# Experts: last four jobs written out, the first two slot chunks summed into tokens between them, final adds in a row

## The chip, the cores and the metric

One core of one Trainium2 chip runs the whole program. The metric is the device time of one execution in microseconds. The kernel is written by hand, with one instruction stream for each engine: TensorE (PE) multiplies matrices, VectorE (DVE) and ScalarE (ACT) do elementwise work, GpSimd (POOL) does a little, and SyncE (SP) issues nearly all transfers. Semaphores are all that ties the streams together. Matrix products land in eight PSUM banks, called pb[0] to pb[7], and everything else lies in SBUF.

## The reference, condensed to what matters

256 tokens of width 1024 go through two transformer blocks of two layers each. The second block ends each of its two layers (called l = 0 and l = 1) with a mixture of 32 experts, in groups of 8. This is the part that the change touches:

```python
e = grp[:, None] * EXPERTS_PER_GROUP + top_local          # two experts for each of 256 tokens
y_e = (silu(x_e @ w_gate[e]) * (x_e @ w_up[e])) @ w_down[e]   # 1024 -> 512 -> 1024
x = x + sum over the two experts of gate * y_e
```

The weights of one expert are three fp32 matrices of 2 MB each. After l = 0 comes the mixer of the next layer, which begins with a projection of the new x. After l = 1 comes a last rmsnorm, and its result is the output.

Which expert a token gets depends on the inputs. On the inputs of `setup_inputs()`, the reference's router, evaluated by itself, gives these numbers of tokens to experts 0 to 31 (each row sums to 512):

```
l = 0: 16 14 5 8 21 10 9 17 15 14 18 12 16 20 15 10 15 27 15 11 7 21 7 23 15 29 6 29 20 15 32 20
l = 1: 9 13 16 4 14 7 12 17 28 35 39 12 21 20 48 29 5 8 6 10 12 0 6 1 18 8 22 25 14 13 26 14
```

No expert has more than 64, and in l = 1 one expert, number 21, has none.

## The kernel before, in words

**Slots and jobs.** The 512 pairs of token and expert are sorted by expert into 512 slots. A job is one pass of one expert over a window of W = 64 slots that begins at the expert's first slot; what a job writes past its own slots, the next job writes over. `route` counts the tokens of each expert (`cm`), and `wm` is the number of jobs of each of 33 bins (32 experts, and one for what expert 0 has over 64). `wm` starts as "count over 0", or 1 where the bin's number is below `FORCED`, and grows with each further 64 tokens. FORCED = FIXED + 2 = 20: bins 0 to 19 get a job whether or not a token chose them. The sum of `wm`, less a constant, is read into the register `more` on every engine.

**Steps.** In step j PE multiplies job j's window by the gate matrix (`products` with m = 0, in two halves) and by the up matrix (m = 1), turns job j-1's gate and up results (`turn`), turns job j-2's result (`results`), and multiplies job j-1's hidden values by its down matrix (`down`). Order on PE: turn, gate half 0, turn, gate half 1, results, up, down. Steps 0 to 17 (FIXED = 18) are written out, with a planner that lays their weights out in three groups of buffers. Then a loop (`Fori(0, more)`) runs the steps from 18 on, one step more is written out (`step(more, last=True)`), and then comes `end`, in which only the rest of the last jobs is done.

**Weights.** From the loop on, weights go into `raw`, six buffers of 1 MB: one pair for gate, one for up, one for down. SP issues one 2 MB transfer for each matrix (L763), in the order gate, up, down. It issues a gate's after PE has used up the last gate of that pair, and likewise for the others, which the semaphore `used` counts. The last down comes as two transfers of 1 MB (L760, L761), into the gates' pair.

**Slots back to tokens.** The results stand turned in `ysT`. They are turned back in four chunks of 128 slots. For a chunk c: PE turns it in two halves of 4 transposes (`slots_turned(c)`, L1964) into `slot_bank(half, c)`, which is pb[6], pb[7] for c = 0 and c = 1, pb[0], pb[1] for c = 2 and pb[4], pb[5] for c = 3; ACT scales it by the gate values and rounds it (`slots`, L1252); DVE writes the rest that the rounding left (`low_slots`, L2772). Then PE sums the slots into tokens by a product with the 0/1 matrix `selT` (`into_tokens`, L2027), 2 matmuls of 128x512 for each half of the columns, half of the tokens (NT = 2) and chunk, so 8 for a chunk and 32 for a layer. In the kernel before, all four chunks add up in pb[0] to pb[3], and DVE then adds these four banks to `h` (L2808). Chunk 0 is turned at the start of the last step, chunk 1 in it ahead of `down`, chunks 2 and 3 in `end`. All 32 sums stand after the last `down`.

**After that.** In l = 0 PE turns `h` in two halves (`turn_half(8, 0)`, and `turn_half(8, 1)` inside `project` after its first 12 matmuls), DVE makes the low parts of the first mixer weights (`split_to`, L2119) and of the turned `h` (`evac_half`, L2130), and PE goes on with `project` (L1366). In l = 1 ACT squares `h` in four quarters (L1338), POOL makes the root, DVE multiplies by the gain (`with_gain`, L2816) and then by the root (L2862), and three transfers write the output.

## Time and profile before

| | |
|---|---|
| runs of the kernel before | 1877.14, 1872.03, 1872.38 us; median 1872.38 |
| the profiled execution's own time | 1876.49 us |
| its span, first to last instruction | 1874.7 us |
| mean granted TensorE clock | 0.99 |
| PE busy | 1784.4 us, 95% |
| DVE busy | 847.4 us, 45% |
| ACT busy | 705.3 us, 38% |
| moved by transfers | 549.37 MB, mean 293 GB/s |
| share of the chain that ended last | PE 72%, DMA 20%, DVE 4%, ACT 1%, POOL 1%, issue 1% |

The span is the time between the first and the last instruction of one profiled execution, and its own time, 1.8 us more, includes what lies around it. "Busy" of PE is the time in which matmuls were in flight, so a PE that is busy all the time need not be at its peak. The chain that ended last follows the work back from the last instruction, at each step to what released it; what is not on it had time to spare. The experts of l = 0 run from about 847 to 1306 us of the span, those of l = 1 from about 1418 to 1862 us.

### The profile page before, as it was taken

Reading aid. Unit: us, or ns where it says so; the run is one execution under the profiler, and the core shown is the slowest. Engines: PE = TensorE matmul, PEld = TensorE weight load, DVE = VectorE, ACT = ScalarE, POOL = GpSimd, SP = SyncE. Lnnn points to the kernel's source line nnn. Section 1 sums busy time; section 2 is a strip of 40 time slices with the busy share of each in tenths; the row PEclk is TensorE's granted clock in tenths of the full one; section 3 lists DMA queues with packets and bytes.
Section 4 is the critical chain, followed back from the end, with each engine's and each line's share of the span. In section 5 each row is a group of like instructions: output and inputs, shape, how many; then the busy total and the mean of one; then the engine's idle time right before and its main releaser. Section 6 shows DMA issues by size and latency. Waiting matters only on the chain.

```text
span 1874.7 us, 26258 instructions
## 1 busy us (share of the span) xinstructions
PE 1784.4 (95%) x10171; PEld 1142.2 (61%) x10171; DVE 847.4 (45%) x1532; ACT 705.3 (38%) x1205; POOL 105.6 (6%) x148
## 2 busy tenths in 40 slices
PE   8999999998999999999999898889999999988887
PEld 6779998886699997975334333334985334333333
DVE  4766556668765657874111111114785112111113
ACT  5554333656643335543222222223543222222223
POOL 3330000112200000010000000000010000000000
PEclk9999999998999999999999999999999999999999
DMA  9645555552256554558999999999648999999995
GB/s 319 205 155 189 180 180 179 165 184 79 94 166 200 180 180 135 180 224 368 428 428 427 427 421 425 429 428 370 198 171 368 425 427 428 427 426 424 428 429 226
DMA packets 130589, 549.37 MB, mean 293 GB/s; under 512 B 8030, under 2 KB 67768, under 8 KB 103480
## 3 DMA queue, kind: packets, MB, share of 16 engines
q1 hardware_dynamic: 127080, 539.53, 73.4%
q0 software_dynamic: 3088, 8.10, 1.4%
q8 instruction: 70, 1.15, 0.3%
q10 hardware_dynamic: 320, 0.34, 0.1%
q14 instruction: 31, 0.25, 0.0%
HBM read 546.83 MB, written 1.11 MB: 292 GB/s over the span
## 4 chain that ended last, share of the span: by engine, by line
PE 72%; DMA 20%; DVE 4%; ACT 1%; POOL 1%; issue 1%; SPq 0%; POOLq 0%; DVEq 0%; ACTq 0%
PE pb L1366 29%; DMA raw<-in_w_expert_down 16%; PE pb L1928 12%; PE pb L1955 10%; PE pb L1661 6%; DMA spare<-in_w_expert_gate 3%; PE pb L1936 2%; PE pb L1495 1%; PE pb L1472 1%; PE pb L1518 1%; PE pb L1595 1%; PE pb L1945 1%; POOL rms L903 1%; DVE parts L2119 1%; PE pb L1378 1%
## 5 line engine op out<-in xcount | busy, mean ns | idle before, releaser
L2119 DVE TENSOR_TENSOR parts<-raw,parts 128x2048 fp32r<-128x2048 f32 (+1 forms) x138 | 307.2, 2232 | 109.2 <-ACT parts L923 106.3
L923 ACT ACTIVATE parts<-raw 128x2048 fp32r<-128x2048 f32 (+1 forms) x138 | 256.5, 1867 | 210.5 <-PE pb L1366 154.1
L1366 PE MATMUL pb<-xT,parts 128*128 128x256 f32 (+1 forms) x2712 | 333.3, 283 | 0.0
L1366 PEld LDWEIGHTS pb<-xT,parts 128*128 128x128 f32 (+1 forms) x2712 | 329.2, 191 | 4.7 <-issue 2.9
L1928 PE MATMUL pb<-raw,xw 128*64 128x512 f32 x1360 | 319.5, 601 | 11.6 <-DMA raw<-in_w_expert_gate 11.6
L2739 DVE TENSOR_TENSOR qk<-qk,pb 128x256 f32<-128x256 f32 x126 | 53.1, 421 | 585.2 <-ACT qk L1235 585.0
L1366 PE MATMUL pb<-parts,xT 128*128 128x512 f32 (+1 forms) x1200 | 272.7, 386 | 3.0 <-DVE xT L2130 1.5
L1366 PEld LDWEIGHTS pb<-parts,xT 128*128 128x128 f32 x1200 | 218.4, 190 | 49.3 <-issue 4.4
L1230 ACT ACTIVATE qk<-pb 128x512 f32<-128x512 f32 x126 | 75.2, 597 | 302.8 <-PE pb L1928 302.8
L1928 PEld LDWEIGHTS pb<-raw,xw 128*64 128x64 f32 x1360 | 86.8, 136 | 153.7 <-issue 125.2
L1955 PE MATMUL pb<-raw,qk 128*64 128x512 f32 x624 | 142.8, 596 | 30.7 <-DMA raw<-in_w_expert_down 30.7
L1936 PEld LDWEIGHTS pb<-cst,qk 128*128 128x128 f32 x504 | 70.5, 209 | 97.3 <-issue 97.3
L1661 PE MATMUL pb<-parts,hidT 128*128 128x512 f32 x528 | 124.3, 391 | 3.1 <-DVE hidT L2356 3.1
L1955 PEld LDWEIGHTS pb<-raw,qk 128*64 128x64 f32 x624 | 47.1, 136 | 120.0 <-issue 119.7
L1928 PE MATMUL pb<-spare,xw 128*64 128x512 f32 x464 | 111.8, 614 | 4.8 <-DMA spare<-in_w_expert_gate 4.8
L1661 PEld LDWEIGHTS pb<-parts,hidT 128*128 128x128 f32 x528 | 97.7, 188 | 23.3 <-DVE hidT L2356 3.9
L1235 ACT ACTIVATE qk<-pb 128x256 f32<-128x256 f32 x126 | 48.3, 383 | 167.1 <-PE pb L1936 162.7
L1246 ACT ACTIVATE qk<-pb 128x512 f32<-128x512 f32 x63 | 37.6, 597 | 167.4 <-PE pb L1955 167.4
L1936 PE MATMUL pb<-cst,qk 128*128 128x128 f32 x504 | 93.5, 309 | 0.0
L2755 DVE COPY work<-pb 128x512 f32 x63 | 43.6, 692 | 62.1 <-PE pb L1945 62.1
L1955 PE MATMUL pb<-spare,qk 128*64 128x512 f32 x272 | 61.7, 594 | 4.6 <-DMA spare<-in_w_expert_down 4.6
L1928 PEld LDWEIGHTS pb<-spare,xw 128*64 128x64 f32 x464 | 30.0, 138 | 54.0 <-issue 45.9
(335 smaller groups left out, 1583.0 us busy)
## 6 DMA issues: line engine op xcount, KB each, us to landing
raw<-in_w_expert_gate SPq DMA_DIRECT2D x41, 2048.0 KB, 10.0
raw<-in_w_expert_up SPq DMA_DIRECT2D x37, 2048.0 KB, 10.8
raw<-in_w_expert_down SPq DMA_DIRECT2D x35, 2048.0 KB, 10.7
spare<-in_w_expert_down SPq DMA_DIRECT2D x16, 2048.0 KB, 15.9
spare<-in_w_expert_up SPq DMA_DIRECT2D x14, 2048.0 KB, 16.5
raw<-in_w_ffn_gate SPq DMA_DIRECT2D x22, 1024.0 KB, 5.3
raw<-in_w_ffn_up SPq DMA_DIRECT2D x22, 1024.0 KB, 5.3
raw<-in_w_ffn_down SPq DMA_DIRECT2D x22, 1024.0 KB, 4.9
```

What stands on the lines that cost most here:

```text
L923: nc.scalar.activation(parts[:, (SPL0[seg] + k) % SPL, 0, 0:kk * nn], raw[:, place, 0:kk * nn], ACT.Copy).then_inc(hi_done[seg], 1)
L1230: nc.scalar.activation(dst, pb[bank][:], ACT.Copy).then_inc(done[l], 1)
L1235: nc.scalar.activation(dst.rearrange("p (k s) -> p k s", k=4), pb[2 + m][:].rearrange("p (k i s) -> p k i s", k=4, i=2)[:, :, 0, :], ACT.C ...
L1246: nc.scalar.activation(ys, pb[4][:], ACT.Copy).then_inc(ys_done[l], 1)
L1366: ins = mm(out_ap, b if flip else a, a if flip else b, start=first and n == 0, stop=last and n == 2)
L1661: ins = mm(pb[2 * c + t][:], hidT[:, j, i, P * t:P * (t + 1)], w[p][:, j, 512 * c:512 * (c + 1)], start=(q == 1 and j == 0 and n == 0), st ...
L1928: ins = mm(pb[m][rows, :], xw[:, 4 * hf + k, :], w[:, k, :], start=(hf == 0 and k < 2), stop=(hf == 1 and k >= 2))
L1936: ins = nc.tensor.transpose(pb[2 + m][:, P * q:P * (q + 1)], view(src, q, [[DE // P, P]]), ident)
L1955: ins = mm(pb[4][W * c:W * (c + 1), :], ehj[:, 2 * hf + k, :], w[:, k, 512 * c:512 * (c + 1)], start=(hf == 0 and k == 0), stop=(hf == 1 a ...
L2119: v.tensor_tensor(two[:, 1, :], raw[:, place, 0:kk * nn], two[:, 0, :].bitcast(F32), ALU.subtract)\
L2739: v.tensor_tensor(d, d, pb[2 + m][:].rearrange("p (k i s) -> p k i s", k=4, i=2)[:, :, 1, :], ALU.add)\
L2755: v.tensor_copy(ysT2[:, :, :, bass.ds(s0, W)], pb[6][:].rearrange("p (q c s) -> p c q s", q=4, c=2))\
```

## The change

- `REST = 4` steps are written out behind the loop (before: one), on SP, ACT, PE and DVE. `more` is smaller by 3 for the same number of jobs. `FORCED` becomes FIXED + REST + 1 = 23.
- In the four steps, numbered 0 to 3: step 0 turns chunk 0 at its start, step 1 sums it; step 2 turns chunk 1 at its start, step 3 sums it. `TURNS` and `SUMS` hold this.
- New on PE, `sums(sc, half)`: 4 matmuls for one half of the columns of chunk sc, into pb[5] and pb[7]. Half 0 stands ahead of the step's `down`, half 1 behind it; half 1 of chunk 1 stands in `end`, between `down`'s second half and `slots_turned(2)`. Each waits until DVE has added the one before it.
- New on DVE, `add_part(sc, half)`: two adds of 128x512 from pb[5] and pb[7] into `h`, at the end of the step (half 1 of chunk 1 after `hidden` of `end`).
- `slots_turned(1)` waits in addition until both parts of chunk 0 are added, because pb[7] serves both.
- `into_tokens` covers chunks 2 and 3 alone (16 matmuls): chunk 2's first half around `results(end, 1)`, then `slots_turned(3)`, then chunk 3.
- The four final adds stand in a row. In l = 0 `split_to` and `evac_half`, which stood between the second and the third, come after the fourth. In l = 1 `with_gain(0)`, which stood between the third and the fourth, comes after the fourth.

```diff
-FORCED = FIXED + 2
+REST = 4
+FORCED = FIXED + REST + 1
...
+        TURNS, SUMS = {0: 0, 2: 1}, {1: 0, 3: 1}
...
+                for ahead in range(1, REST):
+                    job_weights((more, ahead))
+                end = (more, REST)
...
+                def sums(sc, half):
+
+                    pe.wait_ge(yt_v, 8 * l + 2 * sc + 2)
+                    if sc or half:
+                        pe.wait_ge(part_added, 4 * l + 2 * sc + half)
+                    for t in range(NT):
+                        for i in range(2):
+                            ins = mm(pb[5 + 2 * t][:], selT[:, sc, P * t:P * (t + 1)],
+                                     y_slots(half)[:, i, 512 * sc:512 * (sc + 1)], start=(i == 0), stop=(i == 1))
+                    ins.then_inc(sums_ready, 1)
+
...
-                    if last:
+                    if turned_chunk is not None:
                         pe.wait_ge(yadd_done[l], at(j, 1, -1))
-                        slots_turned(0)
+                        if turned_chunk:
+                            pe.wait_ge(part_added, 4 * l + 2)
+                        slots_turned(turned_chunk)
...
-                    if last:
-                        pe.wait_ge(yadd_done[l], at(j, 1, 0))
-                        slots_turned(1)
+                    if summed is not None:
+                        sums(summed, 0)
                     down(j, 1, down_at(False), range(1 if last else 2))
+                    if summed is not None and not last:
+                        sums(summed, 1)
...
-                step(more, last=True)
-                end = (more, 1)
+                for n in range(REST):
+                    step((more, n), TURNS.get(n), SUMS.get(n), n == REST - 1)
+                end = (more, REST)
                 turn(end, 1, 0, gs, gs_done)
                 turn(end, 1, 1, us, us_done)
-                down(more, 1, down_at(False), range(1, 2))
+                down((more, REST - 1), 1, down_at(False), range(1, 2))
+                sums(1, 1)
+                pe.wait_ge(yadd_done[l], at(end, 1, -1))
                 slots_turned(2)
-                pe.wait_ge(yt_v, 8 * l + 4)
                 results(end, 2)
                 down(end, 1, down_at(True))
...
                 for t in range(NT):
-                    into_tokens(0, t, 0)
+                    into_tokens(0, t, 2)
                 results(end, 1)
-                for sc in (1, 2):
-                    for t in range(NT):
-                        into_tokens(0, t, sc)
+                for t in range(NT):
+                    into_tokens(1, t, 2)
                 pe.wait_ge(yadd_done[l], at(end, 1, 1))
                 slots_turned(3)
-                for sc in range(3):
-                    into_tokens(1, 0, sc)
-                for t in range(NT):
-                    into_tokens(0, t, 3)
-                for sc in range(3):
-                    into_tokens(1, 1, sc)
+                for half in range(2):
+                    for t in range(NT):
+                        into_tokens(half, t, 3)
                 if l == 0:
                     turn_half(8, 0)
-                into_tokens(1, 0, 3)
-                into_tokens(1, 1, 3)
...
+                def add_part(sc, half):
+
+                    dve.wait_ge(sums_ready, 4 * l + 2 * sc + half + 1)
+                    if sc:
+                        dve.wait_ge(part_added, 4 * l + half + 1)
+                    for t in range(NT):
+                        hh = h[:, t, 512 * half:512 * (half + 1)]
+                        ins = v.tensor_tensor(hh, hh, pb[5 + 2 * t][:], ALU.add)
+                    ins.then_inc(part_added, 1)
...
-                add(0, 0)
-                add(0, 1)
+                for c in range(2):
+                    for t in range(NT):
+                        add(c, t)
...
```

## Rows read from the trace of the kernel before

**Rows 1.** GB/s moved in each fortieth of the span, 46.9 us each.

```profile
GB/s 319 205 155 189 180 180 179 165 184 79 94 166 200 180 180 135 180 224 368 428 428 427 427 421 425 429 428 370 198 171 368 425 427 428 427 426 424 428 429 226
```

**Rows 2.** Windows: us, busy by engine (instructions), clock, DMA share, GB/s.

```profile
1598.00:1831.00 233.00, 208.75 (x962) 77.01 (x958) 36.72 (x80) 56.54 (x113) 0.00 (x0) 0.99 1.01 426
```

**Rows 3.** Line L1230, two per job, in the experts of l = 0.

```profile
L1230 ACT ACTIVATE qk<-pb x64: 597/597/598, 854.3 to 1289.4; 128x512 f32<-128x512 f32 x64
```

**Rows 4.** The same line in the experts of l = 1.

```profile
L1230 ACT ACTIVATE qk<-pb x62: 597/597/599, 1425.4 to 1845.2; 128x512 f32<-128x512 f32 x62
```

**Rows 5.** Chain that ended last, two jobs of the written-out steps: start, us, what.

```profile
970.11 3.58 PE pb L1928 x16
...
982.80 3.58 PE pb L1928 x16
```

**Rows 6.** Timeline of SP: start, us, engine line; last regular jobs of l = 1.

```profile
1820.58 0.33 SPq L763 DMA_DIRECT2D raw<-in_w_expert_down  x1
1826.23 0.34 SPq L763 DMA_DIRECT2D raw<-in_w_expert_gate  x1
1830.26 0.33 SPq L763 DMA_DIRECT2D raw<-in_w_expert_up  x1
```

**Rows 7.** Page, DMA issues: KB each, median us to landing.

```profile
raw<-in_w_ffn_down SPq DMA_DIRECT2D x22, 1024.0 KB, 4.9
```

**Rows 8.** Timeline of PE, l = 1, last three steps and end: [idle before].

```profile
1820.34 0.75 PE L1936 MATMUL pb<-cst,qk 128*128 128x128 f32 x4
1821.56 1.94 PE L1928 MATMUL pb<-raw,xw 128*64 128x512 f32 x8 [0.48 <-DMA raw<-in_w_expert_gate]
...
1826.56 3.65 PE L1928 MATMUL pb<-raw,xw 128*64 128x512 f32 x16
1831.45 3.65 PE L1955 MATMUL pb<-raw,qk 128*64 128x512 f32 x16 [1.23 <-DMA raw<-in_w_expert_down]
1835.03 1.09 PE L1964 MATMUL pb<-cst,work 128*128 128x128 f32 x8
...
1836.54 1.94 PE L1928 MATMUL pb<-raw,xw 128*64 128x512 f32 x8
...
1846.15 1.94 PE L1955 MATMUL pb<-raw,qk 128*64 128x512 f32 x8
...
1857.12 0.60 PE L1945 MATMUL pb<-cst,qk 128*128 128x128 f32 x4
...
1859.41 1.03 PE L1964 MATMUL pb<-cst,work 128*128 128x128 f32 x8
1860.20 4.84 PE L2027 MATMUL pb<-parts,selT 128*128 128x512 f32 x20
```

**Rows 9.** Timeline of DVE, l = 1, end.

```profile
1857.86 0.69 DVE L2755 COPY work<-pb 128x512 f32 x1 [3.29 <-PE pb L1945]
...
1862.35 1.28 DVE L2808 TENSOR_TENSOR h<-h,pb 128x512 f32<-128x512 f32 x2 [0.17 <-PE pb L2027]
...
1865.41 1.22 DVE L2816 TENSOR_TENSOR qk<-h,qk 128x1024 f32<-128x1024 f32 x1
...
1869.45 0.75 DVE L2862 TENSOR_SCALAR xs<-qk,rms 128x1024 f32<-128x1024 f32 x1 [0.96 <-POOL rms L903]
```

**Rows 10.** Timeline of ACT, l = 1: squares of h.

```profile
1867.27 0.63 ACT L1338 ACTIVATE xs<-h 128x512 f32<-128x512 f32 x1 [1.13 <-DVE h L2808]
```

**Rows 11.** Chain that ended last, from the end of l = 0 into the mixer.

```profile
1306.47 1.28 DVE h L2808 x2
1307.75 2.20 DVE parts L2119
1309.95 1.58 DVE xT L2130 x4
...
1311.58 3.00 PE pb L1366 x12
...
1315.46 13.93 PE pb L1366 x84
```

More of the change, by code:

```diff
@@ L1278, in moe @@
                     step(j)
-                step(more, last=True)
-                end = (more, 1)
-                slots(1)
+                for n in range(REST):
+                    step((more, n), TURNS.get(n))
+                end = (more, REST)
                 first_parts(end, 1, 0, eg)
@@ L2012, in moe @@
                     step(j)
-                step(more, last=True)
-                end = (more, 1)
+                for n in range(REST):
+                    step((more, n), TURNS.get(n), SUMS.get(n), n == REST - 1)
+                end = (more, REST)
                 turn(end, 1, 0, gs, gs_done)
                 turn(end, 1, 1, us, us_done)
-                down(more, 1, down_at(False), range(1, 2))
+                down((more, REST - 1), 1, down_at(False), range(1, 2))
+                sums(1, 1)
+                pe.wait_ge(yadd_done[l], at(end, 1, -1))
                 slots_turned(2)
-                pe.wait_ge(yt_v, 8 * l + 4)
                 results(end, 2)
@@ L2027, in into_tokens @@
                         ins = mm(pb[2 * half + t][:], selT[:, sc, P * t:P * (t + 1)],
-                                 y_slots(half)[:, i, 512 * sc:512 * (sc + 1)], start=(sc == 0 and i == 0),
+                                 y_slots(half)[:, i, 512 * sc:512 * (sc + 1)], start=(sc == 2 and i == 0),
                                  stop=(sc == 3 and i == 1))
@@ L2773, in low_slots, with step @@
                             .then_inc(yt_v, 1)
-                def step(j, last=False):
+                def add_part(sc, half):
[6 more added lines that the diff above has]
+                    ins.then_inc(part_added, 1)
+                def step(j, turned_chunk=None, summed=None, last=False):
                     later = not isinstance(j, int) or j > 1
-                    if last:
-                        low_slots(0)
+                    if turned_chunk is not None:
+                        low_slots(turned_chunk)
                     if not later and j:
@@ L2787, in step @@
                         to_slots(j, 2)
+                    if summed is not None:
+                        add_part(summed, 0)
+                        if not last:
+                            add_part(summed, 1)
                 for j in range(FIXED):
@@ L2794, in moe @@
                     step(j)
-                step(more, last=True)
-                end = (more, 1)
-                low_slots(1)
+                for n in range(REST):
+                    step((more, n), TURNS.get(n), SUMS.get(n), n == REST - 1)
+                end = (more, REST)
                 sums(end, 1)
-                hidden(end, 1, at(more, 6, 4))
+                hidden(end, 1, at((more, REST - 1), 6, 4))
+                add_part(1, 1)
                 low_slots(2)
```

55 lines of the change are left out of this document (26 added, 29 removed).

## The prediction

> **What bounds the kernel now.** I read four views, from coarse to fine. The slices of the page come first: in both expert parts the GB/s row stands flat at 421 to 429 [rows 1], and the window over the late jobs of l = 1 gives 426 GB/s with all sixteen engines' share full, while PE is busy for 209 of 233 us [rows 2]. So the transfers bound this stretch. An early job, whose weights were loaded ahead, shows what PE needs by itself: the up products begin at 970.11 and again at 982.80, so 12.69 us a job [rows 5]. A late job takes 14.70 us: `down` begins at 1831.45 and then at 1846.15 [rows 8]. One job's weights are 3 x 2.097 = 6.29 MB, and at 426 GB/s that is 14.8 us, the same number. PE has 2.0 us to spare in a late step, and the timeline shows where: 1.23 us idle ahead of `down`, 0.48 us ahead of the first gate product and some more inside the turn before it, all released by a transfer [rows 8].
>
> The end of a layer is different. From 1831.45 on PE is hardly idle, and from 1856 to 1865 it only turns and sums slots [rows 8]. DVE's adds follow, then the squares, the root and the output [rows 9, 10]. So there are two kinds of place: steps in which PE's work is free up to 2.0 us, and an end in which it is paid.
>
> **The largest part: one more job.** FORCED goes from 20 to 23, so bins 20, 21 and 22 get a job even when no token chose them. The trace gives the jobs of each layer: line L1230 runs twice a job, 64 times in l = 0 and 62 times in l = 1 [rows 3, 4], so 32 and 31 jobs. With at most 64 tokens an expert, 31 jobs means one expert of 20 to 31 without a job. The trace doesn't say which; the reference's router says 21, with 0 tokens. It is now forced, and l = 1 has 32 jobs. l = 0 keeps its 32. The new job's window is written over by the next, so it only costs time: 6.29 MB in a stretch that the transfers bound. There is no cover for it, since the row of GB/s has no gap in it. I take 14.7 us. The lower bound is PE's 12.69 us [rows 5]; it would hold only if the transfers were ahead. The upper bound from the slowest full slice, 421 GB/s [rows 1], is 14.9 us.
>
> The Trainium skill (DMA: Bandwidth & Descriptors, Specifications) gives about 358 GB/s as a core's limit from HBM. By it the job would cost 17.6 us. The trace disagrees, with 426 GB/s held for 233 us [rows 2].
>
> **Steps 0 to 2, written out.** A step out of the loop issues the same transfers in the same order, and PE's written-out steps run at 12.69 us without a gap [rows 5], so being written out costs nothing. The moved work is what counts.
>
> Step 0 turns chunk 0 first. The kernel before does the same in its last step, and there the gate products begin 1.51 us after `down`'s end (1835.03 to 1836.54) instead of 1.22 (1820.34 to 1821.56) [rows 8]: 0.3 us late, which the 1.23 us ahead of `down` swallows. Cost 0.
>
> Step 1 sums half of chunk 0 ahead of `down`. Twenty such matmuls take 4.84 us [rows 8], so four take 0.97; this fits into the 1.23 us. The other half comes behind `down` and is followed at once by step 2's turning of chunk 1, which waits until DVE has added that half, since both use pb[7]. So PE goes through 0.97 (sums), 1.28 (two adds, as two take [rows 9]), some 0.2 for two handovers (one shows as 0.17 [rows 9]), 1.02 (turning) and 0.49 (the turn of the gates; 1.51 less 1.02): 3.96 us, where steady state begins the gate products after 1.22. Queued behind that wait are all of step 2's products. They start 2.8 us late. About 1.3 us of that goes into the idle time ahead of `down`, so `down` of step 2 is 1.5 us late. In step 3 the gates' idle time of 0.7 takes it to 0.8, and the first sum of chunk 1 adds 0.97 against 1.3: `down` of step 3 is 0.4 us late. Bounds for this: 0 (the handovers overlap) and 2.8 us (no idle time takes any).
>
> **The queue of loads.** SP's gate load of step 2 waits for products that are 2.8 us late. In steady state it is issued at 1826.23 [rows 6], while the `down` transfer issued at 1820.58 still has until about 1831.3 to land. A 1 MB load with nothing before it lands in 4.9 us [rows 7]; 2.5 of these are its bytes at 426 GB/s, so 2.4 are fixed, and a 2 MB one would need 7.3. Issued at 1829.0 it would land at 1836.3, and the gate products of a steady step begin 14.70 after 1821.56, at 1836.26. So it is just in time, and I take 0; the upper bound is the full 2.8 us.
>
> **What the last step saves.** It loses the turning of two chunks, 2 x 1.02 us. But its `down` began at 1846.15, exactly 14.70 after the one before, although both turnings stood ahead of it [rows 8]: it waited for its weights anyway. So this removal is worth 0, and the 0.4 us of lateness stands.
>
> **The end, up to the adds.** PE is without idle time from here. `sums(1, 1)` adds 0.97 ahead of `slots_turned(2)`, so the last `down` ends 0.4 + 0.97 = 1.4 us late. `results(end, 1)` keeps four sums ahead of it, and comes 1.4 late too. DVE's copy then ended at 1858.55 [rows 9] and ends at 1859.95; the last chunk is turned behind it. Before, PE was still busy with eight sums until 1859.41 [rows 8], so the turning moves by only some 0.45 us. From there on the old kernel's first adds, at 1862.35, came 0.17 us after DVE had ended its last `low_slots` [rows 9]: DVE's chain, not PE, set them. They move by the same 0.45. The sixteen removed sums, 16 x 0.24 = 3.9 us, are thus mostly work that hid behind DVE and ACT. Bounds: 0.45 later and 2.5 us earlier (3.9 less 1.4).
>
> **The adds in a row, l = 0.** Before: two adds, the split (2.20), the evacuation (1.58), and PE's `project` begins at 1311.58 and then has no gap for 18 us [rows 11]. Now two more adds, 1.4 us, stand ahead of the split. So `project` begins 0.45 + 1.4 = 1.85 us later, and all behind it moves. Bounds: -2.5 and +3 us.
>
> **The adds in a row, l = 1.** Before, the fourth add came after `with_gain(0)`, which takes 1.22 [rows 9], and the last square began at 1867.27 [rows 10]. Now the adds run from 1862.8 to 1865.5, squares start after the second at 1864.1, and at 0.63 each [rows 10] the last of four starts at 1866.0. Both gains end near 1868.0, when the root is ready too. The end comes 1.3 us earlier. Bounds: -3 and +0.5 us.
>
> **Sum.** 14.7 + 1.85 - 1.3 = +15.2 us. The profiled execution took 1876.49 us and would take 1891.7. It lies 4.1 us above the median of the runs, 1872.38, and one of the three was at 1877.14; the forecast is for the median: 1887.6 us.
>
> **Rivals.**
> - No extra job: `FORCED` has no effect on this input, as when the empty bin of l = 1 isn't among 20 to 22. For it: the trace alone leaves 12 experts open, and 9 of these give 31 jobs again. Against it: the router's counts, which agree with 32 and 31 jobs in both layers [rows 3, 4]. It decides whether the run is slower at all: 1872.4 + 0.55 = 1872.9 us. Chance 6%.
> - Late loads open a gap: the 2.8 us of step 2 pass through the queue of transfers in both layers. For it: the estimate left no margin. Against it: three pairs of buffers, and a `down` transfer between. 1887.6 + 5.6 = 1893.2 us. Chance 10%.
> - The end is PE's after all, and the sixteen sums come off in full, 2.5 us in both layers: 1872.4 + 14.7 - 5.0 = 1882.1 us. For it: PE's row at the end is solid [rows 8]. Against: the 0.17 us behind `low_slots` [rows 9]. Chance 7%.
> - The extra job's transfers are slower than their neighbours', by a limit on what one core reads. The rows bound it to 14.9 us, and so 1887.8; the 6.29 MB would have to meet something that 426 GB/s held for 233 us did not. Chance 2%, inside the range. By the skill's 358 GB/s (same page and section) the time would be 1890.5.
>
> **How the numbers follow.** The forecast holds 75%. Its own range goes from 1884.5 (bounds of the ends) to 1892.5 (runs at the level of 1877.14). With the late loads it reaches 1894. Left out are the first and third rival and a remainder, about 17%. About 0.3%, 5.6 us, is what a measurement of this kernel can tell from no change: faster 2%, within it 5%, slower 93%.
>
> **What would show it.** Line L1230 of l = 1 must count 64 instead of 62, and gate, up and down issues one more each. PE must stand idle some 1.5 us ahead of step 2's turning, released by DVE's add, and begin the gate products of step 2 some 2.8 us late; `down` of step 3 must be within 0.5 us of its steady place. SP's gate load must not leave a gap in the GB/s. From the last add to `project` there must be the split and the evacuation in l = 0, and in l = 1 four adds without a gap. The prediction falls if l = 1 still has 31 jobs, or if the cadence of the loop isn't 14.7 us.

## The result, and the profile after

The changed kernel is slower, as forecast, and by more than forecast.

| comparison | changed kernel | kernel before | ratio, 95% interval |
|---|---|---|---|
| first | 1897.31 us (4 runs) | 1873.51 us (4 runs) | 1.012 [1.0106, 1.0134] |
| second | 1897.69 us (4 runs) | 1875.96 us (19 runs) | 1.0115 [1.0098, 1.0132] |

The forecast was 1887.6 us in a range that began at 1884.5 and reached 1894 with late loads, so the medians lie 3.3 to 3.7 us above its upper end. Between the kernels lie 23.8 us by the first comparison, 21.7 us by the second, and 21.6 us between the two profiled executions (1898.06 less 1876.49 us). The forecast difference was 15.2 us.

**The additional job is there.** Line L1240 of the changed kernel (L1230 before) in the experts of l = 1, to compare with [rows 4]:

```profile
L1240 ACT ACTIVATE qk<-pb x64: 597/598/601, 1431.2 to 1867.3; 128x512 f32<-128x512 f32 x64
```

64 instead of 62, so 32 jobs.

**The written-out steps of l = 1.** The timeline of PE, to compare with [rows 8]. L1965 is `down`, L1985 the new sums, L1974 the turning of slots, L1938 the gate and up products:

```profile
1822.86 3.65 PE L1965 MATMUL pb<-raw,qk 128*64 128x512 f32 x16 [0.94 <-DMA raw<-in_w_expert_down]
...
1827.67 1.94 PE L1938 MATMUL pb<-raw,xw 128*64 128x512 f32 x8 [0.48 <-DMA raw<-in_w_expert_gate]
...
1836.44 1.19 PE L1985 MATMUL pb<-parts,selT 128*128 128x512 f32 x4
1837.85 3.65 PE L1965 MATMUL pb<-raw,qk 128*64 128x512 f32 x16 [0.22 <-DMA raw<-in_w_expert_down]
1841.43 1.20 PE L1985 MATMUL pb<-parts,selT 128*128 128x512 f32 x4
1844.10 1.07 PE L1974 MATMUL pb<-cst,work 128*128 128x128 f32 x8 [1.47 <-DVE h L2802]
...
1845.58 1.94 PE L1938 MATMUL pb<-raw,xw 128*64 128x512 f32 x8
...
1868.60 1.94 PE L1965 MATMUL pb<-raw,qk 128*64 128x512 f32 x8 [0.20 <-DMA raw<-in_w_expert_down]
...
1875.94 3.65 PE L1965 MATMUL pb<-raw,qk 128*64 128x512 f32 x16
```

Step 1 begins its gate products 4.81 us after the `down` before (1822.86 to 1827.67). In step 2 it is 7.73 us (1837.85 to 1845.58), 2.9 us more, with 1.47 us idle ahead of the turning, released by DVE's add. The first half sum did fit ahead of `down`: only 0.22 us of the wait is left. Between these two lines lies `down` of step 2, with no idle time ahead of it:

```profile
1854.06 3.60 PE L1965 MATMUL pb<-raw,qk 128*64 128x512 f32 x16
```

It comes 16.21 us after that of step 1, so 1.5 us late. So far it went as forecast. But `down` of step 3 doesn't catch up: it waits for its weights until 1868.60, which is 30.75 us after that of step 1, where two steady jobs take 29.4.

SP's timeline, and windows of 1 us with the columns of [rows 2], show what happened in between:

```profile
1842.00 0.34 SPq L767 DMA_DIRECT2D raw<-in_w_expert_down  x1
1850.25 0.34 SPq L767 DMA_DIRECT2D raw<-in_w_expert_gate  x1
```

```profile
1850.00:1851.00 1.00, 1.00 (x8) 0.60 (x8) 0.21 (x1) 0.60 (x1) 0.00 (x0) 1.00 0.41 164
1851.00:1852.00 1.00, 1.00 (x8) 0.37 (x6) 0.48 (x1) 0.00 (x0) 0.00 (x0) 1.00 1.37 279
1852.00:1853.00 1.00, 1.00 (x8) 0.34 (x6) 0.00 (x0) 0.00 (x0) 0.00 (x0) 1.00 0.54 213
```

The gate load, for step 3, is issued 8.25 us after the `down` load, against 5.65 in steady state [rows 6], and the stream falls to half. Against 426 GB/s the three windows lack 262, 147 and 213 GB/s for 1 us each: 622 KB, or 1.5 us of transfers. `down` of step 3 is late by about as much.

**Into the mixer after l = 0.** The chain that ended last, PE's timeline at its first row, and the window over it (clock, share of the transfer engines and GB/s at the end of the row), to compare with [rows 11]. `project` is L1376 here:

```profile
1314.92 5.38 PE pb L1376 x12
...
1321.18 13.96 PE pb L1376 x84
```

```profile
1314.92 5.38 PE L1376 MATMUL pb<-parts,xT 128*128 128x512 f32 x12 [3.88 <-DVE xT L2150]
```

```profile
1314.90:1320.00 5.10, 5.08 (x12) 4.01 (x13) 2.17 (x1) 0.00 (x0) 0.00 (x0) 0.50 0.90 279
```

In the kernel before, the same twelve matmuls took 3.00 us, with less idle time ahead of them:

```profile
1311.58 3.00 PE L1366 MATMUL pb<-parts,xT 128*128 128x512 f32 x12 [1.52 <-DVE xT L2130]
```

Now PE has been idle for 3.88 us ahead of them, and they run at a granted clock of 0.50, so at 1.2 GHz.

**The end of l = 1.** Timelines of DVE and POOL, to compare with [rows 9]:

```profile
1885.12 2.48 DVE L2844 TENSOR_TENSOR h<-h,pb 128x512 f32<-128x512 f32 x4 [0.23 <-PE pb L2053]
1887.71 2.36 DVE L2851 TENSOR_TENSOR qk<-h,qk 128x1024 f32<-128x1024 f32 x2
1891.02 0.75 DVE L2892 TENSOR_SCALAR xs<-qk,rms 128x1024 f32<-128x1024 f32 x1 [0.96 <-POOL rms L913]
```

```profile
1887.87 1.11 POOL L902 TENSOR_SCALAR rms<-rms 128x2 f32<-128x2 f32 x1 [11.79 <-ACT xs L1348]
1889.15 0.97 POOL L907 TENSOR_TENSOR rms<-rms 128x2 f32<-128x2 f32 x1 [0.17 <-ACT xs L1348]
```

In the kernel before, POOL's timeline shows the same two operations, and they take 0.19 and 0.41 us:

```profile
1865.10 0.19 POOL L892 TENSOR_SCALAR rms<-rms 128x2 f32<-128x2 f32 x1 [12.46 <-ACT xs L1338]
1868.14 0.41 POOL L897 TENSOR_TENSOR rms<-rms 128x2 f32<-128x2 f32 x1 [2.86 <-ACT xs L1338]
```

From the first add to the output's scaling it is 5.90 us (1885.12 to 1891.02), against 7.10 before (1862.35 to 1869.45 [rows 9]).

**Where the 21.6 us went**, by the two profiled executions. Each row is the length of a stretch between the same two instructions, in us. "First late `down`" is the one that begins at 1669.92 before and at 1676.03 after:

| stretch | before | after | difference |
|---|---|---|---|
| start of the span to the `down` of l = 0 that is step 0's in the changed kernel | 1231.53 | 1230.74 | -0.8 |
| l = 0, `down` of step 0 to first half of the next-to-last `down` | 58.74 | 60.99 | +2.25 |
| l = 0, from there to the last `down` | 6.36 | 7.33 | +0.97 |
| l = 0, last `down` to `project` | 14.95 | 15.86 | +0.9 |
| l = 0, first twelve matmuls and the turning | 3.88 | 6.26 | +2.4 |
| `project` to the first late `down` of l = 1 | 354.46 | 354.85 | +0.4 |
| l = 1, from there to first half of the next-to-last `down` | 176.23 | 192.57 | +16.3 |
| l = 1, from there to the last `down` | 6.35 | 7.34 | +1.0 |
| l = 1, last `down` to the first add | 9.85 | 9.18 | -0.7 |
| l = 1, first add to the output's scaling | 7.10 | 5.90 | -1.2 |

The first and the sixth row hold work that the change doesn't touch; they are the scatter of single executions. Of the seventh, 14.7 us are the job and 1.6 the steps. Of the second row's 2.25 us and these 1.6, 0.6 and 0.3 us arise in step 1 already, whose `down` comes 15.25 and 14.99 us after that of step 0, before any wait of the new work could act.

### The profile page after: what moved, and what is told of

Read it like the earlier page. It is cut to its first block, busy times and chain, and to the rows that moved or that the text cites. A ratio compares the mean times of both kernels' runs of the same rounds, so it can differ in the third digit from the quotient of the medians.

```text
span 1896.2 us, 26408 instructions
## 1 busy us (share of the span) xinstructions
PE 1801.2 (95%) x10231; PEld 1148.1 (61%) x10231; DVE 859.1 (45%) x1553; ACT 708.7 (37%) x1212; POOL 107.2 (6%) x148
## 3 DMA queue, kind: packets, MB, share of 16 engines
HBM read 553.12 MB, written 1.11 MB: 292 GB/s over the span
## 4 chain that ended last, share of the span: by engine, by line
PE 72%; DMA 19%; DVE 5%; ACT 1%; POOL 1%; issue 1%; SPq 0%; POOLq 0%; DVEq 0%; ACTq 0%
PE pb L1376 28%; DMA raw<-in_w_expert_down 16%; PE pb L1938 13%; PE pb L1965 10%; PE pb L1671 6%; PE pb L1946 2%; DMA extra<-in_w_expert_up 1%; DMA spare<-in_w_expert_gate 1%; PE pb L1505 1%; PE pb L1482 1%; PE pb L1528 1%; PE pb L1605 1%; PE pb L1955 1%; POOL rms L913 1%; DVE parts L2139 1%
## 5 line engine op out<-in xcount | busy, mean ns | idle before, releaser
L1938 PE MATMUL pb<-raw,xw 128*64 128x512 f32 x1392 | 327.0, 601 | 12.1 <-DMA raw<-in_w_expert_gate 10.6
L1376 PE MATMUL pb<-xT,parts 128*128 128x256 f32 (+1 forms) x2712 | 333.3, 283 | 0.0
L1376 PEld LDWEIGHTS pb<-xT,parts 128*128 128x128 f32 (+1 forms) x2712 | 329.2, 191 | 4.7 <-issue 2.9
L1376 PE MATMUL pb<-parts,xT 128*128 128x512 f32 (+1 forms) x1200 | 274.8, 388 | 4.9 <-DVE xT L2150 3.9
L1376 PEld LDWEIGHTS pb<-parts,xT 128*128 128x128 f32 x1200 | 219.7, 191 | 51.5 <-DVE xT L2150 4.1
L1240 ACT ACTIVATE qk<-pb 128x512 f32<-128x512 f32 x128 | 76.5, 598 | 311.0 <-PE pb L1938 311.0
L1938 PEld LDWEIGHTS pb<-raw,xw 128*64 128x64 f32 x1392 | 88.7, 136 | 157.7 <-issue 128.3
L1965 PE MATMUL pb<-raw,qk 128*64 128x512 f32 x640 | 146.3, 596 | 27.5 <-DMA raw<-in_w_expert_down 27.5
L1965 PEld LDWEIGHTS pb<-raw,qk 128*64 128x64 f32 x640 | 48.3, 137 | 118.5 <-issue 118.2
L1938 PE MATMUL pb<-spare,xw 128*64 128x512 f32 x464 | 109.2, 601 | 1.8 <-DMA spare<-in_w_expert_gate 1.8
L1965 PE MATMUL pb<-spare,qk 128*64 128x512 f32 x272 | 61.7, 594 | 4.8 <-DMA spare<-in_w_expert_down 4.8
L1938 PEld LDWEIGHTS pb<-spare,xw 128*64 128x64 f32 x464 | 29.6, 136 | 50.2 <-issue 44.6
## 6 DMA issues: line engine op xcount, KB each, us to landing
raw<-in_w_expert_down SPq DMA_DIRECT2D x36, 2048.0 KB, 10.7
spare<-in_w_expert_up SPq DMA_DIRECT2D x14, 2048.0 KB, 15.2
```

The costliest lines, as they stand in the source:

```text
L1240: nc.scalar.activation(dst, pb[bank][:], ACT.Copy).then_inc(done[l], 1)
L1376: ins = mm(out_ap, b if flip else a, a if flip else b, start=first and n == 0, stop=last and n == 2)
L1938: ins = mm(pb[m][rows, :], xw[:, 4 * hf + k, :], w[:, k, :], start=(hf == 0 and k < 2), stop=(hf == 1 and k >= 2))
L1965: ins = mm(pb[4][W * c:W * (c + 1), :], ehj[:, 2 * hf + k, :], w[:, k, 512 * c:512 * (c + 1)], start=(hf == 0 and k == 0), stop=(hf == 1 a ...
```

## The experiments

The experiments' ratios are against the kernel before on the same chip, with these medians for it: 1876.73 us for the first four, 1875.73 us for the next four, 1875.96 us for the last.

### The extra job, taken out and put in alone

The changed kernel with the forced bins of before:

```diff
-link(v.scalar_tensor_tensor(wm, cm[:, 0:1], 0.0, tri[0:BINS, FORCED:FORCED + 1], ALU.is_gt, ALU.max))
+link(v.scalar_tensor_tensor(wm, cm[:, 0:1], 0.0, tri[0:BINS, 20:21], ALU.is_gt, ALU.max))
```

> The changed kernel, but wm begins at 1 only for bins 0 to 19, as before the change; all else is the changed kernel's. Theory (one more job costs its transfers in full, 14.7 us): L1240 counts 62 in l = 1, the time falls by 14.7 us from the changed kernel's 1897.3 to about 1882.6, and stays 9 us above the kernel before. Rival (the extra time lies in the written-out steps and ends, and the job is partly hidden): it falls by 12.7 us or less, to 1884.6 or more.

Measured: 1882.46 us (10 runs), ratio 1.0032 [1.002, 1.0044]. L1240 counts 62 in l = 1. That is 14.9 us below the first median of the changed kernel, as the theory has it, and 5.7 us above the kernel before. The 9 us that the expectation names beside it rest on the 1873.5 us of the first comparison; here the kernel before had 1876.73. By the differences from the kernel before, the job is 16.0 us (21.7 less 5.7), so the medians alone place it between 14.9 and 16.0.

The kernel before with the job alone:

```diff
-FORCED = FIXED + 2
+FORCED = FIXED + 5
```

> The kernel before, with FORCED = 23 and nothing else. Theory (the job costs 14.7 us wherever it stands): 1873.5 + 14.7 = 1888.2 us. Rival (the job and the moved sums worsen each other): less than 12.7 us more, so under 1886.2.

Measured: 1889.7 us (4 runs), ratio 1.0068 [1.0043, 1.0093], so 13.0 us more, with an interval of 8 to 17. By time alone this doesn't tell 12.7 from 14.7. The chain that ended last does:

```profile
1829.34 3.67 PE pb L1955 x16
1844.02 3.65 PE pb L1955 x16
```

The cadence is still 14.68 us a job, and L1230 counts 64 in l = 1. Cadence and count together settle the job: about 14.7 of the 21.7 us. The rest, 6 to 7 us, is the four steps' and the ends'.

### The clock ahead of `project`

```diff
                 if l == 0:
                     turn_half(8, 0)
+                    spin(8)
```

> The changed kernel with eight matmuls of ones (256 columns, into pb[7], results unused) after turn_half(8, 0) in l = 0, in the 3.9 us in which PE is idle there. Theory (the idle time lets the granted clock fall to 0.50, and project's first twelve matmuls then take 5.4 instead of 3.0 us): the granted clock of those twelve is 1.0, they take 3.0 us, and the time falls by 2.4 us to 1894.9. Rival (something else slows those twelve, such as the weight transfers in the same stretch): they still take 5.4 us, and the time is that of the changed kernel or more.

Measured: 1895.6 us (4 runs), ratio 1.0096 [1.0068, 1.0124]. The timeline of PE:

```profile
1308.79 3.62 PE L1821 MATMUL pb<-cst,ones 128*128 128x256 f32 x16
1312.83 3.02 PE L1376 MATMUL pb<-parts,xT 128*128 128x512 f32 x12 [0.42 <-DVE xT L2151]
1315.69 1.03 PE L1388 MATMUL pb<-cst,h 128*128 128x128 f32 x8
```

With PE kept at work the twelve take 3.02 us, and from their start to the 84 that follow it is 3.89 us instead of 6.26 (3.88 before). Nothing else was changed, and in the four profiled executions with this idle time and no filler (the changed kernel twice, e1 and e4) the twelve took 5.38, 4.58, 4.60 and 5.04 us. So the idle time is what the clock fell for. The weight transfers beside them, the rival's cause, are still there: 336 GB/s over the twelve, at a granted clock of 1.00. The median fell by 1.7 to 2.1 us, against 2.4 expected, which is within its scatter.

### The wait in step 2

```diff
-                    if turned_chunk is not None:
+                    if turned_chunk == 0:
                         pe.wait_ge(yadd_done[l], at(j, 1, -1))
-                        if turned_chunk:
-                            pe.wait_ge(part_added, 4 * l + 2)
-                        slots_turned(turned_chunk)
+                        slots_turned(0)
...
                     products(j, *halves[0])
+                    if turned_chunk:
+                        pe.wait_ge(yadd_done[l], at(j, 1, -1))
+                        pe.wait_ge(part_added, 4 * l + 2)
+                        slots_turned(turned_chunk)
```

> The changed kernel, but step 2 turns chunk 1 after its first gate products instead of ahead of everything, so DVE's add of the second half of chunk 0 runs beside them. Theory (the 1.47 us of waiting and the 1.0 us of turning ahead of the gates make the next loads late and drain the queue of transfers): step 2's gate products begin about 1.8 us after down's end instead of 4.1, the GB/s between the loads of step 2 and 3 stays above 400, and down of step 3 comes 1.3 to 1.7 us earlier in each layer: 2.6 to 3.4 us in all, 1893.9 to 1894.7 us. Rival (the dip in GB/s comes from the written-out steps of SP themselves): the dip and the lateness of step 3 stay, and the time too.

Measured: 1895.71 us (4 runs), ratio 1.0098 [1.0075, 1.012]. The timeline of PE in steps 1 to 3 of l = 1:

```profile
1836.28 3.65 PE L1965 MATMUL pb<-raw,qk 128*64 128x512 f32 x16 [0.22 <-DMA raw<-in_w_expert_down]
...
1841.46 1.94 PE L1938 MATMUL pb<-raw,xw 128*64 128x512 f32 x8
1843.33 1.09 PE L1974 MATMUL pb<-cst,work 128*128 128x128 f32 x8
...
1865.94 1.94 PE L1965 MATMUL pb<-raw,qk 128*64 128x512 f32 x8 [0.18 <-DMA raw<-in_w_expert_down]
```

No idle time stands ahead of the turning, the gate load is issued 6.52 us after the `down` load (1840.44 to 1846.96) instead of 8.25, and from `down` of step 1 to that of step 3 it is 29.66 us instead of 30.75; in l = 0 it is 29.56 (1261.08 to 1290.64) instead of 31.07. That is 1.1 and 1.5 us less, so the lateness came from what stood ahead of the gate products, the wait and the turning behind it. The other runs agree: `down` of step 2 comes 16.20 or 16.21 us after that of step 1 in both layers of all four profiled executions with the old order (the changed kernel twice, e1 and e3), and 14.66 to 14.88 us in those of e4 to e7. That step 3 doesn't make the 1.5 us good is the part of the queue of loads. Its effect on the median, 1.6 to 2.0 us, is under the 2.6 to 3.4 expected, by no more than the scatter. The expectation of over 400 GB/s throughout was missed: of the four windows of 1 us from 1848 on, one stands at 279 and one at 377.

### The row of adds in l = 0, undone and done alone

e4 with the order of before at the end of l = 0 (DVE and PE):

```diff
                 add(0, 0)
                 add(0, 1)
+                if l == 0:
+                    split_to(2, 1)
+                    evac_half(8, 0)
                 add(1, 0)
                 add(1, 1)
...
-                for half in range(2):
-                    for t in range(NT):
-                        into_tokens(half, t, 3)
+                for t in range(NT):
+                    into_tokens(0, t, 3)
                 if l == 0:
                     turn_half(8, 0)
+                for t in range(NT):
+                    into_tokens(1, t, 3)
```

> e4_turn_after_gates0 with the order of the kernel before at the end of l = 0: DVE splits and evacuates between the second and the third add, PE turns h ahead of the last two sums of chunk 3. Theory (two adds in front of the split cost 1.4 us, and the idle time they open lets PE's clock fall for the first twelve matmuls of project, 2.0 us more): from the last down to project 14.4 us instead of 15.8, the twelve matmuls take 3.0 instead of 5.0 us at a granted clock of 1.0, and the time is 3.4 us below that of e4, about 1892.3 us. Rival (the sums of the second half, now behind turn_half, delay the evacuation or the next adds by as much): no change beyond 1 us from e4's 1895.7.

Measured: 1892.9 us (4 runs), ratio 1.0094 [1.0078, 1.0109]. The timeline of PE:

```profile
1293.88 3.65 PE L1965 MATMUL pb<-raw,qk 128*64 128x512 f32 x16
...
1308.60 3.02 PE L1376 MATMUL pb<-parts,xT 128*128 128x512 f32 x12 [0.46 <-DVE xT L2153]
```

From the last `down` to `project` it is 14.7 us instead of 15.86, and the twelve take 3.02 us again. The median fell by 2.8 us against e4 (3.4 expected).

But the clock falls here too, only earlier. Just before, the turning of `h` takes 1.97 us where it took 1.04 before the change, and the window over it and the four sums behind it shows a granted clock of 0.56:

```profile
1304.79 1.97 PE L1388 MATMUL pb<-cst,h 128*128 128x128 f32 x8 [1.37 <-DVE h L2847]
```

```profile
1304.80:1308.00 3.20, 3.20 (x12) 2.71 (x12) 3.20 (x4) 2.04 (x5) 0.00 (x0) 0.56 0.03 9
```

PE has two holes ahead of it, of 1.13 and 1.37 us, where the row of sums was solid in the kernel before. So taking sums away from this end opens idle time even with DVE's order of before. That `project` finds the clock back at 1.00 is partly luck: in e6, which has the same instructions there, the low clock lasts into the twelve, as its window over them shows:

```profile
1309.20:1313.30 4.10, 4.07 (x14) 3.25 (x15) 3.37 (x3) 0.87 (x1) 0.00 (x0) 0.71 0.71 242
```

The same part in the kernel before, and nothing else of the change:

```diff
                 add(0, 0)
                 add(0, 1)
                 if l == 0:
+                    add(1, 0)
+                    add(1, 1)
                     split_to(2, 1)
...
+                into_tokens(1, 0, 3)
+                into_tokens(1, 1, 3)
                 if l == 0:
                     turn_half(8, 0)
-                into_tokens(1, 0, 3)
-                into_tokens(1, 1, 3)
```

> The kernel before with one part of the change alone: in l = 0 the four adds stand in a row ahead of split_to and evac_half, and turn_half(8, 0) follows all sums. l = 1 is that of the kernel before. Theory (two adds ahead of the split cost 1.4 us and open an idle time in which the granted clock falls): project begins 1.4 us later after the last down, its first twelve matmuls take 4.6 to 5.4 us instead of 3.0, and the time is 3 to 3.8 us more, 1879 to 1880 us. Rival (the clock falls only with the shorter tail of sums of the changed kernel, since here PE still works through 20 sums until just before): the twelve take 3.0 us, and only 1.4 us is lost.

Measured: 1880.46 us (10 runs), ratio 1.0021 [1.0011, 1.0031], so 4.5 us more. The timeline of PE, and the window:

```profile
1295.89 3.65 PE L1955 MATMUL pb<-raw,qk 128*64 128x512 f32 x16
...
1313.13 5.49 PE L1366 MATMUL pb<-parts,xT 128*128 128x512 f32 x12 [3.81 <-DVE xT L2130]
```

```profile
1313.10:1318.40 5.30, 5.27 (x12) 4.02 (x13) 2.18 (x1) 0.00 (x0) 0.00 (x0) 0.50 0.89 289
```

The first part of the theory was too small: `project` begins 17.2 us after the last `down`, 2.3 us later than before, not 1.4. DVE also waits 0.99 us for PE's sums ahead of the third add, which begins at 1308.02; before, the split and the evacuation filled that time. The second part holds: 3.81 us of idle time and a clock of 0.50, 2.5 us lost. So the rival falls: the long tail of sums doesn't keep the clock up. In the changed kernel this end costs 3.3 us (0.9 and 2.4 in the table above). That it would cost more without the shorter tail of sums is suggested by the 2.3 us here against the 0.9 there, and no run tests it.

### The order in l = 1, and POOL

```diff
                 add(1, 0)
+                if l:
+                    dve.wait_ge(par2_loaded, 16 * (len(PARS) - NPAR0 + 1))
+                    dve.wait_ge(h_done, 39)
+                    with_gain(0)
                 add(1, 1)
```

> e5_adds_apart_l0 with with_gain(0) between the third and the fourth add in l = 1, as in the kernel before. Theory A (POOL's small operations wait until DVE's with_gain ends: 1.11 and 0.97 us in the changed kernel against 0.19 and 0.41 before): POOL's first operation falls back to 0.2 us, but the second still ends with with_gain(1), so the end of l = 1 moves by less than 0.5 us. Theory B (the row of adds was worth its 1.2 us): the end of l = 1 comes 1.2 us later than in e5.

Measured: 1893.95 us (4 runs), ratio 1.0103 [1.0083, 1.0123]; e5 had 1892.9, which four runs each can't tell apart. The timelines say more. From the first add to the output's scaling it is 6.03 us (1878.49 to 1884.52) against 5.90 in e5 (1875.11 to 1881.01). POOL in e6:

```profile
1881.25 0.51 POOL L902 TENSOR_SCALAR rms<-rms 128x2 f32<-128x2 f32 x1 [11.77 <-ACT xs L1348]
1883.21 0.41 POOL L907 TENSOR_TENSOR rms<-rms 128x2 f32<-128x2 f32 x1 [1.45 <-ACT xs L1348]
```

Theory A stands: the row of adds in l = 1 is worth 0.1 us. POOL's first operation fell to 0.51 us, not to the 0.2 expected; DVE's `with_gain(0)` now began earlier, and the operation again ended just after it. What made the end shorter than before is that the third add no longer waits for PE, 1.06 us in the kernel before. It is PE's earlier sums that gain here, and not DVE's order.

### Are written-out steps free?

The kernel before with four steps written out, `FIXED = 15` so that l = 1 keeps 31 jobs, and no new sums, turnings or adds:

```diff
-FIXED = 18
+FIXED = 15
+REST = 4
-FORCED = FIXED + 2
+FORCED = FIXED + REST + 1
...
-                step(more, last=True)
-                end = (more, 1)
+                for n in range(REST):
+                    step((more, n), last=n == REST - 1)
+                end = (more, REST)
```

> The kernel before with four steps written out instead of one and FIXED = 15 (31 jobs in l = 1, FORCED 20), chunks turned and summed as in the kernel before, the adds too. Theory A (a written-out step has a price of its own: in the changed kernel the down of step 1 came 29.9 us after that two steps earlier instead of 29.4, before any wait could act, with 16 KB of instructions fetched in the same stretch): the same two steps are 0.3 to 1.4 us longer than 29.4 in at least one layer, and loads land 11.0 us or more after their issue instead of 10.7. Theory B (the sums and turnings are the cause): all steps keep 14.7 us a job. In both the time is within 3 us of the kernel before.

Measured: 1877.09 us (10 runs), ratio 1.0005 [0.9996, 1.0015]. The timeline of PE in l = 1 (`down` is L1963, gates L1936), and the share of instruction fetches in the transfers of that stretch:

```profile
1799.33 3.65 PE L1963 MATMUL pb<-raw,qk 128*64 128x512 f32 x16 [1.23 <-DMA raw<-in_w_expert_down]
...
1805.56 1.94 PE L1936 MATMUL pb<-raw,xw 128*64 128x512 f32 x8 [1.90 <-DMA raw<-in_w_expert_gate]
...
1815.28 3.65 PE L1963 MATMUL pb<-raw,qk 128*64 128x512 f32 x16 [1.07 <-DMA raw<-in_w_expert_down]
```

```profile
q8 instruction: 1, 0.02, 0.4%
q14 instruction: 1, 0.01, 0.1%
```

One step takes 15.95 us instead of 14.69, though PE does nothing new in it; in l = 0 one takes 15.63. All other steps keep 14.66 to 14.72, and in these stretches the slowest load lands 11.8 and 12.1 us after its issue instead of 10.9. Theory A stands: a written-out step can be longer by itself, 0.9 and 1.3 us here. In the changed kernel's first profile the same excess is 0.6 us in l = 0 and 0.3 in l = 1, and in the second it is 0.0 and 0.2, so it differs from execution to execution. Four steps aren't needed for it either: the one written-out step of the kernel before takes 15.25 us in e2 and 15.42 in e10, both in l = 0. That the instruction fetch is its cause isn't shown. Such steps have a fetch beside them, but so do steps of 14.69 us in the kernel before (1275.58 to 1290.27) and of 14.68 in the second profile of the changed kernel.

### Two versions without the faults

e5 with three planned steps fewer:

```diff
-FIXED = 18
+FIXED = 15
```

> e5_adds_apart_l0 with FIXED = 15 instead of 18, so FORCED = FIXED + REST + 1 is 20 as before the change and l = 1 has 31 jobs, with the four steps kept. Theory (the extra job is the whole of what FORCED costs, and written-out steps are not faster than loop steps where transfers bound): 14.7 us below e5, about 1877.6 us, within 0.3% of the kernel before on the same chip. Rival (three planned steps fewer drain the loads laid out ahead sooner and cost up to 2 us a job): up to 6 us more, 1883.

Measured: 1877.47 us (10 runs), ratio 1.0006 [0.9995, 1.0018]. 15.4 us below e5, level with the kernel before. Three planned steps fewer cost nothing that the time shows. The profile has longer steps of the kind just described, 16.04 and 16.39 us in l = 0 and 15.39 in l = 1.

The four half sums one to a step, on the changed kernel with the end of l = 0 of e5 and `FIXED = 15`:

```diff
-        TURNS, SUMS = {0: 0, 2: 1}, {1: 0, 3: 1}
+        TURNS, SUMS = {0: 0, 2: 1}, {n: (n // 2, n % 2) for n in range(4)}
...
                     if summed is not None:
-                        sums(summed, 0)
+                        sums(*summed)
                     down(j, 1, down_at(False), range(1 if last else 2))
-                    if summed is not None and not last:
-                        sums(summed, 1)
...
-                sums(1, 1)
```

> e7_fixed15, but the four half sums of chunks 0 and 1 stand one in each of the four steps, always ahead of down, where PE waits for its weights; none stands behind a down or in end, and chunk 1 is turned at the start of step 2, as in the changed kernel, with its wait long satisfied. Theory (a sum of 1.0 us fits the idle time ahead of down, behind down it doesn't): no idle time of PE ahead of the turning, down of step 3 on its place 14.7 us after that of step 2, and the last down 1.0 us earlier than in e7 in both layers, so 2 us below e7 and at or up to 2 us below the kernel before. Rival (the ends are set by DVE's chain, not by the last down): no difference from e7.

Measured: 1874.11 us (11 runs), ratio 0.9995 [0.9986, 1.0004]. The timeline of PE in l = 1:

```profile
1829.00 1.20 PE L1985 MATMUL pb<-parts,selT 128*128 128x512 f32 x4
1830.27 3.65 PE L1965 MATMUL pb<-raw,qk 128*64 128x512 f32 x16
...
1843.65 1.19 PE L1985 MATMUL pb<-parts,selT 128*128 128x512 f32 x4
1844.96 1.94 PE L1965 MATMUL pb<-raw,qk 128*64 128x512 f32 x8
...
1851.31 3.65 PE L1965 MATMUL pb<-raw,qk 128*64 128x512 f32 x16
```

Each sum stands in what was idle time ahead of `down`, `down` of step 3 comes 14.69 us after that of step 2, and from there to the last `down` it is 6.35 us as before the change, instead of 7.34. One step is longer here too, as in e9: step 2 takes 15.34 us, and in l = 0 step 1 takes 15.85. The median is 3.4 us below e7 (2 expected) and 1.6 us below the kernel before; the interval holds 1. So this form costs nothing that can be seen and gains too little to be told from nothing.

### The changed kernel once more

> The changed kernel once more, since its first comparison had four runs and the kernel before has since had a median of 1876 instead of 1873.5 us. From e1 (5.7 us above the kernel before) and the extra job of 14.7 us I expect a ratio of 1.011 and a difference of 20.4 us; the first comparison gave 23.8. If the difference is 22 or more, e1 has missed something that only the two together cost.

Measured: 1897.69 us, 21.7 us more, in the table at the top. That is between the two values named, 20.4 and 22. What only the two parts together could cost is thus about 1.3 us by the medians, which is within their scatter. In its profile `down` of step 3 comes 30.72 and 30.79 us after that of step 1 (l = 0 and l = 1), where the first had 31.07 and 30.75, and the twelve matmuls take 4.58 us.

## Why the prediction was wrong, point by point

**The largest part was right.** One more job in l = 1, 14.7 us, and it decides the sign. e1 took it out (14.9 us), e2 put it in (cadence 14.68 us).

**What the last step saves: right.** Taking the two turnings out gained nothing: in e8 the last step has neither of them, and its `down` in l = 1 still comes 14.69 us after the one before.

**"The queue of loads ... I take 0" was the first step that failed.** The wait itself had the forecast size (1.47 us of idle time, 2.9 us of lateness at the gate products, 1.5 us at `down` of step 2). The estimate for the late gate load left no margin: issued at 1829.0, landing at 1836.3, needed at 1836.26, from a 1 MB load's median. In the run the 2 MB load took some 8.1 us from its issue (1850.25) to the gate products that it released (1858.51, less 0.14 of handover as the chain has it), not 7.3, and the stream lacked 1.5 us of transfers. `down` of step 3 was 1.4 us (l = 1) and 1.7 us (l = 0) late instead of 0.4, where the prediction let the steps' idle time take the lateness up. e4 took the wait out and most of the lateness with it. The rival "late loads open a gap" named this mechanism, priced it at 2.8 us a layer and gave it 10%; it came at about half that price, and together with other terms.

**"Being written out costs nothing" failed too.** It makes 0.6 and 0.3 us of the profiled executions' difference. It was read from the early steps [rows 5], in which weights had been loaded ahead and a load that is a little late harms nobody. In steps that transfers bound, e9 shows 0.9 and 1.3 us for it, the changed kernel 0.0 to 0.6. The cause stays open.

**The adds in a row, l = 0: the idle time that they open was left out.** From the last `down` to `project` +0.9 us was measured, and by the same steps +0.5 was forecast (1.4 for two adds, less 0.9 that the turning of the last chunk gains on the last `down`). What was left out is that PE now has a hole of 3.9 us ahead of `project`, where it had 1.5. The twelve matmuls behind it ran at 1.2 instead of 2.4 GHz, 2.4 us more (1.6 in the second profile). The sum priced this at nothing. e3 fills the hole and brings the 3.0 us back, and e10 produces the loss by the order of the adds alone. e5's 3.02 us show less, since the clock fell there too, ahead of the twelve. The prediction asked of the moved work what DVE does later, and never what PE does meanwhile.

**The end, up to the adds: right in kind.** `sums(1, 1)` cost 0.97 and 0.99 us, and in l = 1 the adds began 0.7 us earlier after the last `down`, where the forecast was 0.9.

**The adds in a row, l = 1: right size, half of it lost, and for another reason.** A gain of 1.75 us from the first add on was forecast, and 1.2 was measured. The prediction had the root ready when DVE's second `with_gain` ends; the timelines have POOL's second operation end only then, and the last one, 0.71 us, and the scaling follow. The missing 0.55 us is put down to that, and no run takes the multiplications away from POOL to test it. And e6 shows that the order of DVE is worth only 0.1 us; the gain came from the third add no longer waiting for PE.

**The sum.** Forecast +15.2. Lateness of steps 1 to 3 beyond 0.4 us: 1.85 in l = 0 (2.25 less 0.4) and 1.2 in l = 1 (1.6 less 0.4), of which 0.6 and 0.3 are the written-out step's and the rest mainly the late loads'. Clock: 2.4. `project`: 0.4. The end of l = 1: 0.75 (0.2 ahead of the adds, 0.55 behind). Together +21.8, against 21.6 between the profiled executions, in which the untouched stretches add -0.4. The first comparison's 23.8 us is more because its median for the kernel before, 1873.51 us, was lower than in all later ones.

The range was too narrow for a plain reason: it let one term reach its bound at a time, while all these small terms lay on the same side, most of them at a place that had been called free.

## What to carry to other kernels

When transfers bound a loop, count for each moved instruction not only whether it fits into PE's idle time but when the next load can be issued: here 1.0 us of sums was free ahead of `down` and cost more than its length behind it, since two adds and a turning queued up behind it and delayed the next load: 1.5 us at the next `down`, in eight layers of eight. A constant such as `FORCED`, changed only so that a loop's count stays positive, can change how much work the inputs cause; work that out from the inputs first. Work taken from an engine at its busiest end, or held up there by another engine's order, can leave a hole that the clock answers.

## What the runs showed of the hardware that I had not expected

- After 3.8 to 3.9 us without a matmul TensorE ran at a granted clock of 0.50 for the next twelve matmuls or most of them (4.58 to 5.49 us in five profiled executions, against 3.00 us). In e3, with 0.42 us of idle time, the same twelve took 3.02 us. The Trainium skill (TensorE: Matmul & The Clock Gate, What's actually happening) says that how busy the engine has lately been decides between two clocks; the trace agrees, with 0.50 and 1.00. Shorter holes can be enough: in e5 and e6, after two of 1.13 and 1.37 or 1.38 us, the turning that follows took 1.97 us instead of 1.04, and the window over it and four sums shows 0.56 and 0.50. In e5 the clock was back at 1.00 for the twelve (3.02 us), in e6 it wasn't yet, though the instructions are the same (4.09 us, 0.71 over them). After holes of 1.13 and 0.98 us the turning took 1.89 us in e8 and 1.09 in e7. What decides between these executions stays open.
- POOL's small operations on 128x2 values took 1.11 and 0.97 us while DVE multiplied two SBUF operands. The first took 0.19 us in the kernel before, beside a DVE add from PSUM. The second took 0.41 us there, and began only 0.36 us before DVE's multiplication ended. Each that ran beside a multiplication ended some 0.05 to 0.1 us after it. The Trainium skill (GPSIMD Engine Reference, Specifications) says that POOL shares its SBUF interfaces with VectorE, with contention where a VectorE instruction has two SBUF inputs; the trace agrees.
- A stretch of code run once, in a place where transfers bound, was 0.2 to 1.7 us longer in some step of most executions, in the same stretch as one or two instruction fetches (0.02 and 0.01 MB). Other steps with such a fetch beside them kept 14.68 or 14.69 us. The Trainium skill (Runtime: NRT & Kernel Launch, Instruction fetch mechanics) has an engine's code streamed by transfers of its own, mostly hidden; here the fetches show beside weight loads that land up to 12.4 us after their issue instead of 10.7 to 10.9. The cause stays open.
